# Expert items: 96 token rows loaded from a DRAM table and transposed, or gathered by a one-hot product

## What is computed

```python
def moe_swiglu(h, w_router, w_gate, w_up, w_down):
    logits = (h @ w_router).astype(jnp.float32)
    top_val, top_idx = lax.top_k(logits, TOP_K)
    weights = jax.nn.softmax(top_val, axis=-1)
    gates = jnp.sum(jax.nn.one_hot(top_idx, N_EXPERTS, dtype=jnp.float32) * weights[..., None], axis=-2)
    out = jnp.zeros_like(h)
    for e in range(N_EXPERTS):
        out = out + gates[..., e:e + 1] * swiglu(h, w_gate[e], w_up[e], w_down[e])
    return out
...
            h = rmsnorm(x, o_norm_ffn[j]) * (1.0 + sc) + sh
            y = moe_swiglu(h, o_router[j], o_exp_gate[j], o_exp_up[j], o_exp_down[j])
            x = x + (g * y).astype(x.dtype)
```

## Time and profile before

| | us |
|---|---|
| Median of 3 runs | 1982.12 |
| Lowest and highest | 1980.96, 1983.53 |
| Profiled execution: span, first to last instruction | 1980.0 |
| Profiled execution: its own time | not given apart |
| PE busy | 1919.8 (97%) |
| DVE, ACT, POOL busy | 689.7, 372.2, 115.0 |
| Mean traffic over the span | 247 GB/s |
| Granted TensorE clock, mean (1 is full) | 0.984 |

### The profile page before, as it was taken

How to read it: one execution, slowest core, us unless ns; L and a number is a source line. 1 busy time by engine, 2 the same in 40 slices (tenths; PEclk the granted TensorE clock), 3 DMA queues, 4 the chain that set the end, 5 groups by cost and what they waited for, 6 DMA issues and landing times.

```text
span 1980.0 us, 28488 instructions
## 1 busy us (share of the span) xinstructions
PE 1919.8 (97%) x11940; PEld 1070.5 (54%) x11940; DVE 689.7 (35%) x1472; ACT 372.2 (19%) x776; POOL 115.0 (6%) x98
## 2 busy tenths in 40 slices
PE   7999999999998999999989988999999999999998
PEld 6577866577865765776756544232323233333332
DVE  3364414354413573434449943010101010101112
ACT  3322102222103232234320012010101010101011
POOL 0000010000010000000016620000000000000000
PEclk9999999999999999999999998999999999999999
DMA  9255574264673316533323135999989999999993
GB/s 359 94 218 208 222 296 170 95 245 182 243 290 128 128 43 246 191 159 128 127 106 126 45 149 202 365 378 376 374 374 375 374 369 382 366 379 364 389 368 143
DMA packets 44037, 483.98 MB, mean 244 GB/s; under 512 B 5108, under 2 KB 6772, under 8 KB 10328
## 3 DMA queue, kind: packets, MB, share of 16 engines
q1 hardware_dynamic: 39136, 471.73, 59.2%
q10 hardware_dynamic: 4248, 9.07, 1.3%
q0 software_dynamic: 576, 2.10, 0.3%
HBM read 479.07 MB, written 10.10 MB: 247 GB/s over the span
## 4 chain that ended last, share of the span: by engine, by line
PE 88%; DVE 6%; DMA 3%; issue 1%; ACT 1%; ACTq 1%; POOL 0%; DVEq 0%; SPq 0%
PE bank L921 20%; PE bank L579 14%; PE bank L951 12%; PE bank L874 8%; PE bank L886 4%; PE bank L738 3%; PE bank L571 3%; PE bank L564 3%; PE bank L744 3%; PE bank L592 2%; PE bank L1000 2%; DMA arena<-bias_rows 1%; PE bank L1095 1%; PE bank L560 1%; PE bank L1028 1%; PE bank L935 1%
## 5 line engine op out<-in xcount | busy, mean ns | idle before, releaser
L921 PE MATMUL bank<-arena 128*32 128x512 f32 x4096 | 457.3, 592 | 0.0
L579 PE MATMUL bank<-arena 128*128 128x256 f32 x1408 | 313.3, 382 | 0.0
L921 PEld LDWEIGHTS bank<-arena 128*32 128x32 f32 x4096 | 136.1, 110 | 300.3 <-issue 300.3
L579 PEld LDWEIGHTS bank<-arena 128*128 128x128 f32 x1408 | 265.5, 190 | 54.2 <-issue 15.8
L951 PE MATMUL bank<-arena 128*32 128x512 f32 x2112 | 238.2, 595 | 0.0
L2077 DVE TENSOR_TENSOR arena<-arena,bank 128x256 f32<-128x256 f32 x64 | 27.0, 421 | 562.1 <-ACT arena L1447 511.6
L874 PE MATMUL bank<-arena 128*128 128x256 f32 x704 | 153.7, 379 | 0.1
L874 PEld LDWEIGHTS bank<-arena 128*128 128x128 f32 x704 | 133.6, 190 | 21.8 <-issue 4.1
L951 PEld LDWEIGHTS bank<-arena 128*32 128x32 f32 x2112 | 62.9, 109 | 133.3 <-issue 132.7
L1447 ACT ACTIVATE arena<-bank 128x256 f32<-128x256 f32 x64 | 24.6, 385 | 517.5 <-PE bank L921 517.4
L2323 POOL TENSOR_TENSOR arena<-arena 128x512 f32<-128x512 f32 x64 | 81.3, 1270 | 293.4 <-DVE arena L2131 290.9
(11 more groups left out here) (446 smaller groups left out, 1894.4 us busy)
## 6 DMA issues: line engine op xcount, KB each, us to landing
arena<-in_wgu SPq DMA_DIRECT2D x88, 2048.0 KB, 10.2
arena<-in_w SPq DMA_DIRECT2D x46, 2048.0 KB, 8.1
arena<-in_wdn SPq DMA_DIRECT2D x88, 1024.0 KB, 9.6
arena<-in_modw SPq DMA_DIRECT2D x24, 2048.0 KB, 9.3
arena<-in_wf SPq DMA_DIRECT2D x11, 3072.0 KB, 10.4
arena<-in_flt_deltas ACTq DMA_DIRECT2D x2, 1024.0 KB, 11.7
slot_rows<-arena ACTq DMA_DIRECT2D x7, 192.0 KB, 3.5
cst<-in_consts SPq DMA_DIRECT2D x1, 1162.0 KB, 7.7
```

The lines of the kernel that those rows point to most:

```text
L579: ins = mm(bank[b][:, j * S:(j + 1) * S], w[:, col:col + P], hT[:, k, :], start=(k == 0), stop=(k == KT - 1))
L921: ins = mm(bank[w % 2][32 * j:32 * j + 32, :], hTe[:, k, TOK * b:TOK * b + TOK], wslot[SLOT[c]][:, k, :], start=(k == 0), stop=(k == KT - ...
```

## The change

- Before the first item DVE computes `token_rows`, now with a third pair of columns: the two plain table rows of each token (`one`, `two`), beside `row2`, in which the rows of the last item are replaced.
- POOL then writes the 256 normed rows of `xn` into the table with four indirect transfers, each token's row to both of its places (`rows_sent`).
- In wave 2 of every item but the last, ACT waits for these four and for the last use of `xin`, and loads the 96 rows of the next item's block into `xin`, a tile that lies over the first half of `xn` (`xin_landed`). The item's own results go to its own block later, as before.
- On PE, `turn_rows` transposes `xin` in 8 blocks of 128x128 at the place where the gather stood. Only the first item is still gathered, ahead of the loop.
- `slots` is left for the first item and, before its first product on DVE, for the last. The result rows are fetched as before, once DVE has signalled `row_of` a second time in the last item.

The core of the diff; left out are a wider `itab`, two renamed semaphores, and reads of PSUM at steps of 128 columns instead of 96:

```diff
--- before.py
+++ after.py
@@ -306,6 +306,7 @@
         hTe = view(W + 16384, KT, SLOTS)
+        xin = view(W, D)
@@ -977,7 +978,7 @@
                 turn(WAVES - 1)
                 if not final:
-                    gather(i + 1)
+                    turn_rows(i)
                 for c in range(FFC):
                     if LAST[c] >= WAVES - 2:
                         down(c)
@@ -992,17 +993,25 @@
-            def gather(i):
-
-                pe.wait_ge(sm["oh_ready"], i + 1)
+            def gather():
+
+                pe.wait_ge(sm["oh_ready"], 1)
                 for j in range(KT):
                     for t in range(TT):
-                        ins = mm(bank[6 + j // 4][:, (j % 4) * SLOTS:(j % 4 + 1) * SLOTS], xn[:, t, j * P:(j + 1) * P],
+                        ins = mm(bank[6 + j // 4][:, (j % 4) * P:(j % 4) * P + SLOTS], xn[:, t, j * P:(j + 1) * P],
                                  oneh[:, t, 64:64 + SLOTS], start=(t == 0), stop=(t == TT - 1))
                 ins.then_inc(sm["ga_ps"], 1)
 
+            def turn_rows(i):
+
+                pe.wait_ge(sm["xin_landed"], i * 16 + 16)
+                for j in range(KT):
+                    ins = nc.tensor.transpose(bank[6 + j // 4][:, (j % 4) * P:(j % 4 + 1) * P], xin[:, j * P:(j + 1) * P], ident)
+                ins.then_inc(sm["ga_ps"], 1)
+
             def turn_slots():
 
+                pe.wait_ge(sm["oh_ready"], 2)
...
@@ -1450,6 +1459,11 @@
                     else:
                         turned(w - 1)
+                    if w == 2 and not final:
+
+                        act.wait_ge(sm["rows_sent"], 16 * 4)
+                        act.wait_ge(sm["ga_ps"], i + 1)
+                        act.dma_start(xin[0:SLOTS, :], a["slots"][i + 1]).then_inc(sm["xin_landed"], 16)
...
@@ -2065,10 +2079,11 @@
             def expert(i, final=False):
 
                 for w in range(WAVES):
-                    if w == 3 and not final:
-                        slots(i + 1)
+                    if w == 0 and final:
+                        slots(i)
                     if w == 2 and final:
-                        token_rows(i)
+                        dve.wait_ge(sm["rows_out"], i * (16 * 3) + 32)
+                        v.memset(small[:, 90:91], 0.0).then_inc(sm["row_of"], 1)
...
@@ -2182,7 +2197,7 @@
-            def token_rows(i):
+            def token_rows():
...
@@ -2208,13 +2223,13 @@
-                dve.wait_ge(sm["rows_out"], i * (16 * 3) + 32)
-                for n, row in enumerate((one, row2)):
+                for n, row in enumerate((one, row2, two)):
                     link(v.tensor_scalar(row, row, 1.0, None, ALU.subtract))
                     ins = v.tensor_copy(itab[:, ITEMS + 2 + 2 * n:ITEMS + 4 + 2 * n], row)
-                    if n == 0:
+                    if n < 2:
                         link(ins)
                 ins.then_inc(sm["row_of"], 1)
+                dve.wait_ge(sm["row_of"], 1)
...
@@ -2280,6 +2295,7 @@
             for n in range(2):
                 v.memset(ysb[:, n, :], 0.0).then_inc(sm["ysb_ready"], 1)
+            token_rows()
             dve.wait_ge(sm["gb_ready"], 4)
             last = last_of(dve)
...
@@ -2327,7 +2343,15 @@
             pool.wait_ge(sm["row_of"], 1)
+            pool.wait_ge(sm["rows_out"], 32)
             table = a["slots"].rearrange("i s d -> (i s) d")
+            for n in (0, 2):
+                for t in range(TT):
+                    at = ITEMS + 2 + 2 * n + t
+                    pool.indirect_dma_start(out=table, in_=xn[:, t, :], in_offset=None,
+                                            out_offset=bass.IndirectOffsetOnAxis(ap=itab[:, at:at + 1], axis=0))\
+                        .then_inc(sm["rows_sent"], 16)
+            pool.wait_ge(sm["row_of"], 2)
             for n in range(2):
                 for t in range(TT):
                     at = ITEMS + 2 + 2 * n + t
```

More of the change, by code:

```diff
@@ L201, in model @@
         small = sb("small", 96)
-        itab = ctx.enter_context(nc.sbuf_tensor("itab", [P, ITEMS + 6], mybir.dt.int32))
+        itab = ctx.enter_context(nc.sbuf_tensor("itab", [P, ITEMS + 10], mybir.dt.int32))
         def view(at, *shape):
@@ L361, in model @@
                 h_ps sil_ready hid_ready dn_ps b5_landed c5_landed s5_step s5_act c5_ready b5_ready b5_ps
-                b5t_ready sv_used sv_ps cz_ready y_out sy_ps gelu_ready glu_ready tb_arg tb_ready iota_ready
-                w_ready z5_ready rt_ps rt_step rt_act items_ready oh_ready ga_ps hte_ready pt_ps pt_ready ysb_ready back_ps low_ready rows_out row_of rows_in stored c_ready
+                b5t_ready rows_sent sv_ps cz_ready y_out sy_ps gelu_ready glu_ready tb_arg tb_ready iota_ready
+                xin_landed z5_ready rt_ps rt_step rt_act items_ready oh_ready ga_ps hte_ready pt_ps pt_ready ysb_ready back_ps low_ready rows_out row_of rows_in stored c_ready
                 x_part nstd_ready hta_ready ystd_ready ysq_ready dn_half
@@ L1116, in _ @@
             pe.wait_ge(sm["gb_ready"], 4)
-            gather(0)
+            gather()
             pe.wait_ge(sm["hta_ready"], 28)
@@ L1510, in _ @@
             for k in range(4, KT):
-                F(hTe[:, k, :], bank[7][:, (k - 4) * SLOTS:(k - 3) * SLOTS], ACT.Identity, scale=small[:, 64 + k:65 + k],
+                F(hTe[:, k, :], bank[7][:, (k - 4) * P:(k - 4) * P + SLOTS], ACT.Identity, scale=small[:, 64 + k:65 + k],
                   bias=mods[:, 72 + k:73 + k]).then_inc(sm["hta_ready"], 1)
@@ L2161, in slots @@
                 v.tensor_scalar(oneh[:, 1, :], places, at[1], None, ALU.is_equal).then_inc(sm["oh_ready"], 1)
-                dve.wait_ge(sm["oh_ready"], i + 1)
+                dve.wait_ge(sm["oh_ready"], 1 if isinstance(i, int) else 2)
             def gathered(i, blocks=KT):
@@ L2166, in gathered @@
                 for k in range(blocks):
-                    ins = v.tensor_scalar(hTe[:, k, :], bank[6 + k // 4][:, (k % 4) * SLOTS:(k % 4 + 1) * SLOTS],
+                    ins = v.tensor_scalar(hTe[:, k, :], bank[6 + k // 4][:, (k % 4) * P:(k % 4) * P + SLOTS],
                                           small[:, 64 + k:65 + k], mods[:, 72 + k:73 + k], ALU.mult, ALU.add)
```

## The result

The changed kernel takes 1963.22 us (median of 4 runs, 1961.45 to 1970.06) against 1982.26 us before (median of 4, 1980.96 to 1983.53). The ratio is 0.9912, with a 95% interval of 0.9896 to 0.9927: 0.9% faster. The forecast was 1963.3 us.

A forecast was written before the change was run, and what follows sets the result against it. The prediction took PE to bound the expert part: seven items saving 2.69 us each give 18.8 us, all else costing 0, so 1982.1 − 18.8 = 1963.3 us. Its own range was 1961.5 to 1966, the range asked for 1960.5 to 1972.5.

The forecast's parts named there:

- Seven gathers, 3.55 us each: On PE, the gathers of all items but the first go, saving 3.55 us each.
- Eight transposes, 0.86 us: On PE, eight transposes come in each of seven items, 0.107 us each, costing 0.86 us an item.
- 18.8 us on PE: Net saving on PE: 3.55 − 0.86 = 2.69 us an item, seven times.
- Row numbers ahead of the loop at no cost: On DVE before the first item: 30 instructions, 6.2 us, covered before its first product is needed; cost 0.
- Writes and wait at no cost: POOL's four indirect writes land between 1242 and 1253 us; ACT's wait in wave 2 costs nothing if landed by 1254.
- The row load at no cost: A 0.39 MB load in each of seven items, issued some 30 us in, needed 60 us later; cost 0.
- would take 1 us, within the 2: If the 0.39 MB met the last gate/up chunk: 1 us, against that chunk's margin of 2 us.
- Copies: Copies of turned rows to SBUF keep their size; start and need move up together, 4.4 us between them stays.
- dear transposes: Rival: PE's transposes don't overlap, 2.18 us for eight; 9.6 us saved, 1972.5 us; chance 0.05.
- a pace set by transfers: Rival: DMA engines set the item period, so added loads and table lengthen the run to 1995.2 us; chance 0.05.
- The late table: Rival: indirect writes land after 1265.7 us, stalling ACT and PE us for us; at 1275, 1972.6 us; chance 0.03.

The follow-up runs named there:

- twofold run: The changed kernel, but with each of the eight blocks transposed twice into the same place, 16 transposes an item: 1969.41 us, ratio 0.9941.

## Why the prediction was right

The time, 1963.22 against 1963.3, agrees better than the runs do among themselves (1961.45 to 1970.06); that closeness is luck, and what counts are the terms.

1. *Seven gathers, 3.55 us each.* Right: with all else kept, 3.92 us with the turns are still there, and the period returns to 94.0.
2. *Eight transposes, 0.86 us.* Right: 0.88. The twofold run gives 0.87 for eight more. The difference of two like places was the right price, and the length of 273 ns in the group row was not. The Trainium skill (TensorE: Matmul & The Clock Gate, Part 4) gives some 275 ns for a transpose of 128 by 128; the trace agrees with it as a length (272 to 273 ns), but back to back one more costs 0.109 us.
3. *18.8 us on PE.* 94.04 − 91.33 = 2.71 us an item against 2.69; 19.0 over the seven places, 18.2 to 19.3 from the first gather to the end.
4. *Row numbers ahead of the loop at no cost.* Right, 4.4 us to spare before DVE's first product could start anyway.
5. and 6. *Writes and wait at no cost.* Right. They landed within 10.3 us, sooner than the 11.1 to 22.4 taken from the reads of before, and the place where a late table would stop PE was the turn of wave 3.
7. *The row load at no cost.* Right in wave 2, but by a weaker argument than stated. The margin, read from a late item, holds for the late ones (1.6 to 2.0 us). The first item was not looked at: there it was about 1 us before the change and is nothing after it. And the added remark that the 0.39 MB, if they did arrive beside the last chunk, "would take 1 us, within the 2" is wrong: in wave 5 they delayed it by 2.0 us. In wave 2 they delay the chunk beside them by as much (12.6 us to landing in the third item where it was 10.4 before, issued at 1434.33 and 1432.57), but nothing waits for it. What saved the step is the pause in the traffic between wave 2 and the last chunk, in which the queue catches up: the down chunk issued there at 1459.9 lands after 4.8 us, 4.7 before.
8. *Copies.* They keep their place: done at 1310.57 + 3.27 = 1313.84 us, needed at 1318.20, 4.4 us as before.

Of the rivals, dear transposes and a pace set by transfers are refuted for this kernel. The late table is a real mechanism, with the edge at the turn where it was put, though 1.6 us ahead of it and not 0.8; the change is some 25 us away from it (landed by 1246.7, turn at 1273.69).

## What to carry over

Where one engine runs without gaps, a change is worth what that engine no longer does, and the price of an added step is best taken as the difference between two places of the trace that differ by just that step, since instruction lengths overlap. Put an added transfer where the queue still has a pause ahead of the tightest load: in wave 2 it was free, in wave 5 it cost. Price it by how much later its neighbour lands, not by its size. Where transfers meet, look at the first pass of the loop on its own; its margins are not those of the later ones.

## What was not expected of the hardware

- Four indirect writes of 128 rows of 4 KB landed within 3.5 to 10.3 us of issue, 11.8 to 24.0 beside the weights, and 3.5 to 4.1 with the queue idle: six times apart for the same transfer.
- The 0.39 MB row load took 10.7 to 11.6 us beside the weights, and beside the last chunk it delayed it by 2.0 us, twice its own 0.95; 1.80 MB there delayed it by 3.2 to 3.6 us, less than their own 4.3.
- After PE had stood still for 14.33 us, the granted clock over the next 5.6 us was 0.50, the lower of its two levels (1.2 GHz of 2.4), and full after that. Even a stop of 3.17 us was followed by a slower stretch, 0.68 over 4.5 us.
- Eight transposes of 96 rows and columns take 0.76 us, of 128 rows and columns 0.97.
